# The opening of a hybrid convolution and S5 block: pole constants ahead of x, two modulation slabs summed on GpSimd, two input tiles run channel by channel

## The chip, the cores and the metric

One core of one Trainium2 chip runs the whole kernel. The metric is device time in microseconds (us); lower is better. The median of three runs of the kernel before is 2548.56 us (2545.19 to 2549.18).

## The reference, cut to what matters

```python
c_act = silu(c)
sh1, sc1, g1, sh2, sc2, g2 = split(c_act @ w_ada + b_ada, 6)   # w_ada: 1024 x 6144
h = rmsnorm(x, norm1_g) * (1 + sc1) + sh1                     # x: 2048 x 1024
z = h @ w_in                                                  # to conv, S5 and gate inputs
...
# S5 mixer: constants of each of 32 groups x 64 states
dt = exp(log_dt); mag = exp(dt * a_re)
e_re, e_im = mag * cos(dt * a_im), mag * sin(dt * a_im)
q_re = ((e_re - 1) * a_re + e_im * a_im) / (a_re ** 2 + a_im ** 2)
q_im = (e_im * a_re - (e_re - 1) * a_im) / (a_re ** 2 + a_im ** 2)
bb_re, bb_im = q_re * b_re - q_im * b_im, q_re * b_im + q_im * b_re
x_re, x_im = scan(e_re, e_im, u @ bb)
y_ssm = glu(gelu(x_re @ c_re - x_im @ c_im + d * u))
...
x = x + g1 * (merged @ w_out)                                 # then a SwiGLU FFN and a last rmsnorm
```

Only the part before the first `h @ w_in` (the "opening", the first 60 us or so) is touched. What it must deliver is h for the first 512 tokens, which needs sh1 and sc1 (the first 2048 columns of `c_act @ w_ada`) and the normalized x, and the constants of the S5 mixer.

## The kernel before, in words

The five engines each run a program of their own, in the order in which it is written, and wait for each other on semaphores; nothing is reordered. `Steps` only gives names to semaphore counts. The sequence is worked in four blocks of 512 tokens, and every fp32 product in the projections is made of three fp32r matmuls (`three`): weight and activation are split into a high and a low part. The weights come in chunks of 128 x 1024, through three `raw` buffers; GpSimd splits each into `w_hi` and `w_lo` (a CAST and a subtraction) in one of two slots.

The opening works as follows.

- SP loads eight slabs of `w_ada` of 1 MB each (`SLABS`; slab n holds shift or scale, one half of the 1024 columns, one half of the 1024 rows), then the first three weight chunks, then small things (`load_small`). ACT's queue loads small vectors (`nat_v`), the four tiles of x (`xs`), the S5 poles (`nat_a`), `log_dt`, and B (`nat_b`).
- The modulation is `c_act @ w_ada`, a vector times a matrix. For slabs 1, 3, 5, 6 and 7 PE does it (`modulation_rows`: four fp32 matmuls a slab, into the rows of bank 7). For slabs 0, 2 and 4 DVE sums row by row (`slab_sum`, four instructions a slab, each scaling a 128 x 512 piece by c and adding it to `acc`), and PE adds up the partitions of these sums with two more matmuls (L1800). DVE then copies the rows (`modrow`, L684), PE transposes them (`mt`), and DVE makes `mod` and `scale`.
- ACT takes squares of x (`norm_stats`), the root, and scales x (`nx`).
- DVE makes the arguments of exp, sin and cos for the S5 constants (`jexp`, `jarg`: fifteen short instructions, each waiting for the one ahead of it through `link`), ACT makes exp and sin of them, and DVE works out q in eleven more.
- PE transposes x in eight channel tiles (`h0` to `h7`, four 128 x 128 transposes each); ACT makes `h_hi` and h in the bank (`h_tile`, two instructions a tile), and DVE makes `h_lo` (`h_split`). Then PE starts the first input tile `us0`, all eight channel tiles of it, then `us1`, `us2`, `us3` and the others.
- After the last `h_split` DVE turns B into the scaled B (seven instructions, L727 to L734) and builds `wm` (24 instructions, L739 to L741), which PE needs only after `ug0`, the sixth tile.
- When a tile `us` is done, ACT copies it (`ssm_input`), stores it, and issues eight DMAs for its turned form (`ssm_turn`), in the order us0, us1, turn 0, us2, turn 1, us3, turns 2 and 3, and only then the sigmoid of `ug0` and the copies of the transposed `wm` (`state_matrix`).

## Time and profile before

| | us |
|---|---|
| median of three runs | 2548.56 |
| the profiled execution, its own time | 2551.3 |
| its span | 2549.5 |
| PE busy | 2492.0 (98% of the span) |
| POOL (GpSimd) busy | 1733.5 (68%) |
| DVE busy | 1641.1 (64%) |
| ACT busy | 863.8 (34%) |

The granted TensorE clock has a mean of 0.993 of full speed over the span. PE is busy nearly all the time after the opening, so the table says that the end is set by when PE can start and by what it then has to do. The opening is short and has little PE work that counts: there, which engine waits for which has to be read instruction by instruction. A row of the timeline gives start and duration, engine, line, operation, tiles (out<-in), and in brackets how long the engine sat idle before it and what ended that. `PEld` is the weight load that goes with a matmul. An fp32 matmul shows as two records.

### The profile page before, as it was taken

The page shows a single profiled execution, that of the slowest core. Times are in us where ns is not written, and L with a number is a line of the kernel's source. Part 1 is how long each engine was busy: PE and PEld are TensorE (multiplying, and loading weights), DVE is VectorE, ACT ScalarE, POOL GpSimd, SP SyncE. Part 2 cuts the span into 40 slices and gives each one's busy share as a digit, 9 for nine tenths or more (in the row PEclk, how much of TensorE's full clock was granted, in tenths as well). Part 3 has the DMA queues.
Part 4 walks back from the last instruction along what each step waited for, and adds up shares of the span by engine and source line. Part 5 has one row for each costly group of instructions (what it writes and reads, how often), then busy time and mean ns, then how long its engine had stood idle before and what let it go on. Part 6 is the DMA issues. An engine that isn't in the chain of part 4 may idle for free. (4 is left out here: it accounts for less than half of the span.)

```text
span 2549.5 us, 31364 instructions
## 1 busy us (share of the span) xinstructions
PE 2492.0 (98%) x11419; PEld 2050.3 (80%) x11419; DVE 1641.1 (64%) x2045; ACT 863.8 (34%) x1367; POOL 1733.5 (68%) x1188
## 2 busy tenths in 40 slices
PE   7999999999999999999999999999999999999998
PEld 3888788888888888887788888878888888887886
DVE  5889739945596648947733334385655336889597
ACT  4322411143012421145333345442323334445444
POOL 2776777677866777676887767787787764445444
PEclk9999999999999999999999999999999999999999
DMA  8676347553656347562332232324565337476433
GB/s 279 203 192 215 108 157 223 156 169 107 221 167 190 124 160 220 136 226 83 124 93 81 79 110 93 108 80 152 174 196 184 111 98 251 129 234 205 156 99 116
DMA packets 426161, 395.66 MB, mean 155 GB/s; under 512 B 92232, under 2 KB 330520, under 8 KB 424472
## 3 DMA queue, kind: packets, MB, share of 16 engines
q1 hardware_dynamic: 324112, 317.83, 40.1%
q10 hardware_dynamic: 101896, 75.82, 9.6%
q8 instruction: 92, 1.51, 0.2%
q14 instruction: 61, 0.50, 0.1%
HBM read 317.88 MB, written 67.24 MB: 151 GB/s over the span
## 5 line engine op out<-in xcount | busy, mean ns | idle before, releaser
L2181 POOL TENSOR_TENSOR w_lo<-raw,w_hi 128x1024 fp32r<-128x1024 f32 x192 | 479.4, 2497 | 15.4
L2179 POOL CAST w_hi<-raw 128x1024 fp32r<-128x1024 f32 x192 | 211.8, 1103 | 369.9 <-PE bank L1865 278.4
L1863 PE MATMUL bank<-h_hi,w_hi 128*128 128x512 f32 x896 | 352.2, 393 | 0.9 <-ACT wm L1296 0.9
L1865 PE MATMUL bank<-h_hi,w_lo 128*128 128x512 f32 x896 | 349.8, 390 | 0.0
L1864 PE MATMUL bank<-h_lo,w_hi 128*128 128x512 f32 x896 | 349.5, 390 | 0.0
L829 DVE SCALAR_TENSOR_TENSOR bank<-uc,cwt,bank 128x512 f32<-128x512 f32 x464 | 323.2, 751 | 6.2
L2204 POOL TENSOR_TENSOR fw_lo<-fsum,fw_hi 128x512 fp32r<-128x512 f32 x176 | 235.8, 1343 | 74.1 <-ACT fw_hi L1573 74.0
L1863 PE MATMUL bank<-xc_hi_T,fw_hi 128*128 128x512 f32 x704 | 275.5, 391 | 4.9 <-DVE tr L1024 3.0
L2231 POOL TENSOR_TENSOR ow_lo<-raw,ow_hi 128x512 fp32r<-128x512 f32 x116 | 165.3, 1427 | 162.7 <-ACT ow_hi L1614 162.6
L1865 PE MATMUL bank<-xc_hi_T,fw_lo 128*128 128x512 f32 x704 | 274.2, 389 | 0.0
L1864 PE MATMUL bank<-xc_lo_T,fw_hi 128*128 128x512 f32 x704 | 274.0, 389 | 0.0
L2110 PE MATMUL bank<-ow_hi,hid_hi 128*128 128x512 f32 x616 | 241.3, 392 | 6.2 <-POOL ow_lo L2231 6.2
L2111 PE MATMUL bank<-ow_hi,hid_lo 128*128 128x512 f32 x616 | 241.0, 391 | 0.0
L2112 PE MATMUL bank<-ow_lo,hid_hi 128*128 128x512 f32 x616 | 240.8, 391 | 0.0
L1863 PE MATMUL bank<-xc_hi_B,fw_hi 128*128 128x512 f32 x528 | 207.2, 392 | 5.1 <-DVE xc_lo_B L813 2.4
L2204 POOL TENSOR_TENSOR fw_lo<-raw,fw_hi 128x512 fp32r<-128x512 f32 x110 | 157.9, 1436 | 77.7 <-ACT fw_hi L1573 77.4
L1864 PE MATMUL bank<-xc_lo_B,fw_hi 128*128 128x512 f32 x528 | 206.0, 390 | 0.0
L1865 PE MATMUL bank<-xc_hi_B,fw_lo 128*128 128x512 f32 x528 | 206.0, 390 | 0.0
L1863 PEld LDWEIGHTS bank<-h_hi,w_hi 128*128 128x128 f32 x896 | 169.0, 189 | 36.0 <-issue 1.7
L1865 PEld LDWEIGHTS bank<-h_hi,w_lo 128*128 128x128 f32 x896 | 168.7, 188 | 35.9
L1864 PEld LDWEIGHTS bank<-h_lo,w_hi 128*128 128x128 f32 x896 | 169.0, 189 | 34.5
L1573 ACT ACTIVATE fw_hi<-fsum 128x512 fp32r<-128x512 f32 x176 | 110.8, 629 | 224.1 <-PE bank L1865 114.5
(333 smaller groups left out, 5220.4 us busy)
## 6 DMA issues: line engine op xcount, KB each, us to landing
raw<-in_w_in SPq DMA_DIRECT2D x112, 512.0 KB, 3.9
raw<-in_w_ffn_in SPq DMA_DIRECT2D x66, 512.0 KB, 5.8
hid_scratch<-tr SPq DMA_DIRECT2D x88, 256.0 KB, 3.2
raw<-tsum_scratch SPq DMA_DIRECT2D x66, 256.0 KB, 3.2
g2b<-in_w_ada SPq DMA_DIRECT2D x64, 256.0 KB, 3.7
ssm_m<-vk_scratch SPq DMA_DIRECT2D x32, 512.0 KB, 5.1
raw<-in_ssm_glu SPq DMA_DIRECT2D x32, 512.0 KB, 3.6
raw<-in_w_out SPq DMA_DIRECT2D x32, 512.0 KB, 3.6
```

Source lines behind the costliest of these rows:

```text
L829: ins = v.scalar_tensor_tensor(out=dst, in0=src, scalar=w, in1=conv_bank(m)[:], op0=ALU.mult, op1=ALU.add)
L1573: s.activation(fw_hi[i][:], src, ACT.Copy).then_inc(whi_done, 1)
L1863: t.matmul(dst, wh, xh, start=first, stop=False)
L1864: t.matmul(dst, wh, xl, start=False, stop=False)
L1865: return t.matmul(dst, wl, xh, start=False, stop=last)
L2110: t.matmul(dst, hid_hi[h][:, cols], ow_hi[w][:], start=(k == 0), stop=False)
L2111: t.matmul(dst, hid_lo[h][:, cols], ow_hi[w][:], start=False, stop=False)
L2112: ins = t.matmul(dst, hid_hi[h][:, cols], ow_lo[w][:], start=False, stop=(k == KH2 - 1))
L2179: g.tensor_copy(hi[:], src[:]).then_inc(hi_done, 1)
L2181: g.tensor_tensor(lo[:], src[:], hi[:].bitcast(F32), ALU.subtract).then_inc(split_done, 1)
L2204: g.tensor_tensor(fw_lo[i][:], part[WEIGHTS[i]], fw_hi[i][:].bitcast(F32), ALU.subtract)\
L2231: g.tensor_tensor(ow_lo[n % OW][:], fraw[n % 4][:, 0:HALF], ow_hi[n % OW][:].bitcast(F32), ALU.subtract)\
```

## The change

Six things are done together.

1. On ACT's queue x is loaded last: poles, `log_dt` and B come first.
2. On SP's queue slabs 6 and 7 are moved behind the first two weight chunks.
3. [...] DVE sums slabs 4 and 6. PE multiplies slabs 1, 3, 5 and 7 only, and slab 7 last, behind the two sum rows.
4. DVE works out the S5 constants before anything of the modulation, then slab 4, the mean for the norm, the first two instructions of B, the root, slab 6, and the rest of B; then `modrow`, `mod` and `scale`. ACT makes exp and sin ahead of the squares of x. PE transposes poles and B early.
5. `us0` and `us1` run together, channel tile by channel tile: for each k PE waits for `h_lo` of k, transposes tile k + 2 (the transposed tiles now use two banks), and does the six matmuls of k. The `h_split` instructions stand between those for `wm`.
6. The third weight chunk is split into a third slot, since the first two are now in use until both tiles end.

The diff, cut to its core:

```diff
+        w_hi += early(ync_at, mc_at, ("w_hi_third", [P, CH], F32R))
+        w_lo += early(ync_at + 4096, mc_at, ("w_lo_third", [P, CH], F32R))
+        slot_of = lambda b, w: SPL if (b, w) == (0, 2) else w % SPL
...
-        pe_pro = ["v1", "ada1", "v0", "ada3", "ada5", "ada6", "ada7", "sums", "mt"] + h_steps[0:4] + ["bx"] + h_steps[4:] + ["v2"]
+        pe_pro = ["v1", "v0", "ada1", "bx", "ada3", "ada5", "sums", "ada7"] + h_steps[0:2] + ["mt"] + h_steps[2:] + ["v2"]
...
-        act_pro = ["cs", "dt"] + norm_act + [f"nx{i}" for i in R(TT)] + ["ej", "m8", "sj", "cj"] + h_act
+        act_pro = ["cs", "dt", "ej", "m8", "sj", "cj"] + norm_act + [f"nx{i}" for i in R(TT)] + h_act
...
-            slab_sum(0)
-            slab_sum(2)
-            norm_mean("pro")
-            slab_sum(4)
-            norm_root("pro")
...
+            slab_sum(4)
+            norm_mean("pro")
...
             dve.wait_ge(*tensor.after("pro", "bx"))
             link(v.tensor_tensor(b1[:], first, by_h(qr), ALU.mult))
             link(v.tensor_tensor(ptmp[:], first, by_h(qi), ALU.mult))
+            norm_root("pro")
+            slab_sum(6)
...
                 link(v.tensor_tensor(wm[:, :, s, :], first, by_h(jer[:, j, :]), ALU.mult))
+                if 1 <= s <= 4:
+                    h_split("pro", 2 * s - 2)
                 link(v.tensor_tensor(part, second, by_h(jei[:, j, :]), ALU.mult))
+                if 1 <= s <= 4:
+                    h_split("pro", 2 * s - 1)
...
             modulation_rows(1)
+            parameter_rows()
             modulation_rows(3)
+            modulation_rows(5)
+            pe.wait_ge(slab_pool, 2 * KD - 1)
+            t.matmul(bank[7][0:4, :], one_row[:, 3:7], acc[:, 0:HALF], start=False, stop=False)
+            pe.wait_ge(pro_v, mark["slab6"])
+            t.matmul(bank[7][0:4, :], one_row[:, 2:6], acc[:, HALF:], start=False, stop=False)\
+                .then_inc(*tensor.step("pro", "sums"))
+            modulation_rows(7)
...
+                    for k in R(KD):
+                        pe.wait_ge(*vec.after("pro", f"hl{k}"))
+                        if k + 2 < KD:
+                            transposes("pro", k + 2)
...
+                        for m in R2:
...
+                            ins = three(bank[plan[b, f"us{m}"]][:], hi[:, k, :], lo[:, k, :], h_hi[:, k, :], h_lo[:, k, :],
+                                        k == 0, k == KD - 1)
...
+            def slab_sum(*slabs):
+
+                sums, made = acc[:, 0:HALF], 0
+                for n in slabs:
+                    pool.wait_ge(ada_in[n], 16)
+                    for j in R(KD // 2):
+                        k = SLABS[n][2] * KD // 2 + j
+                        row = ada[n][:, j, :]
+                        g.tensor_tensor(sums if k == 0 else row, row, cact[:, k:k + 1].broadcast_to([P, HALF]), ALU.mult)\
+                            .then_inc(slab_pool, 1)
+                        made += 1
+                        if k:
+                            pool.wait_ge(slab_pool, made)
+                            g.tensor_tensor(sums, sums, row, ALU.add).then_inc(slab_pool, 1)
+                            made += 1
...
+            slab_sum(0, 2)
...
+            for n in R(6):
+                load_slab(n)
...
                     load(b, n, key)
+                    if b == 0 and n == 1:
+                        load_slab(6)
+                        load_slab(7)
```

How this moves the instructions is seen best in three places. The first is PE from its first transpose to its first weight matmul; `ada` is a slab, `xs` is x, `acc` holds the summed slabs. Before:

```order
L1777 MATMUL bank<-ident,nat_v 128x84
L1788 MATMUL bank<-ada_225,zc 4x512 x4
L1777 MATMUL bank<-ident,nat_a 128x64
L1788 MATMUL bank<-ada_227,zc 4x512 x4
L1788 MATMUL bank<-ada_229,zc 4x512 x4
L1788 MATMUL bank<-ada_230,zc 4x512 x4
L1788 MATMUL bank<-ada_231,zc 4x512 x4
L1800 MATMUL bank<-acc,one_row 4x512 x2
L1805 MATMUL bank<-ident,modrow 128x4 x4
L1818 MATMUL bank<-ident,xs 128x128 x16
```

With the change:

```order
L1779 MATMUL bank<-ident,nat_a 128x64
L1792 MATMUL bank<-ada_227,zc 4x512 x4
L1801 MATMUL bank<-ident,nat_b_205 128x32 x16
L1801 MATMUL bank<-ident,nat_b_206 128x32 x16
L1792 MATMUL bank<-ada_229,zc 4x512 x4
L1792 MATMUL bank<-ada_231,zc 4x512 x4
L1810 MATMUL bank<-acc,one_row 4x512
L1812 MATMUL bank<-acc,one_row 4x512
L1792 MATMUL bank<-ada_233,zc 4x512 x4
L1825 MATMUL bank<-ident,xs 128x128 x8
L1833 MATMUL bank<-ident,modrow 128x4 x4
```

One slab of four matmuls is gone, the last slab stands behind both sum rows, and B's transposes fill a place further up.

The second is DVE between the S5 constants and `modrow`, with the change (`sv` holds the constants, 128 x 32 each; before, `modrow` stood right behind the `jarg` instructions and the slabs ahead of them):

```order
L614 SCALAR_TENSOR_TENSOR jarg<-jarg 128x288
...
L703 TENSOR_TENSOR sv<-sv 128x32
L669 TENSOR_SCALAR acc<-ada_230,vt 128x512
L671 SCALAR_TENSOR_TENSOR acc<-ada_230,vt,acc 128x512 x3
L627 TENSOR_SCALAR ss<-ss 128x4
L716 TENSOR_TENSOR b_216<-bank,sv 128x512
L717 TENSOR_TENSOR ptmp<-bank,sv 128x512
L632 RECIPROCAL rs<-sd 128x4
L671 SCALAR_TENSOR_TENSOR acc<-ada_232,vt,acc 128x512 x4
```

Fifteen instructions stand between the first row and the second, and everything that PE's sum row and ACT's norm wait for now stands behind all of them.

The third is GpSimd behind its constants, with the change (before, the first of these rows was the CAST of chunk 0):

```order
L2182 TENSOR_TENSOR acc<-ada_226,vt 128x512
L2182 TENSOR_TENSOR ada_226<-ada_226,vt 128x512
L2187 TENSOR_TENSOR acc<-acc,ada_226 128x512
...
L2187 TENSOR_TENSOR acc<-acc,ada_228 128x512
L2219 CAST w_hi_52<-raw_49 128x1024
L2221 TENSOR_TENSOR w_lo_54<-raw_49,w_hi_52 128x1024
L2219 CAST w_hi_53<-raw_50 128x1024
L2221 TENSOR_TENSOR w_lo_55<-raw_50,w_hi_53 128x1024
L2219 CAST w_hi_third<-raw_51 128x1024
L2221 TENSOR_TENSOR w_lo_third<-raw_51,w_hi_third 128x1024
```

Fifteen instructions now come ahead of the first split, and three splits follow one another where two did.

## Rows read from the trace of the kernel before

**Rows 1.** Timeline of PE in the opening: start us, us, operation [idle before].
```profile
22.51 16.63 PE L1788 MATMUL bank<-ada,zc 128*4 128x512 f32 x32 [4.69 <-DMA ada<-in_w_ada]
38.97 1.88 PE L1800 MATMUL bank<-acc,one_row 128*4 128x512 f32 x4
...
42.03 1.96 PE L1818 MATMUL bank<-ident,xs 128*128 128x128 f32 x16
```

**Rows 2.** Windows: stretch, length, busy of PE, PEld, DVE, ACT, POOL, PEclk, DMA share, GB/s.
```profile
22.50:28.50 6.00, 5.99 (x8) 0.86 (x8) 2.66 (x5) 3.75 (x6) 0.00 (x0) 0.54 1.04 377
28.70:40.80 12.10, 12.10 (x29) 2.32 (x28) 4.88 (x18) 8.26 (x10) 5.33 (x4) 1.00 0.93 294
```

**Rows 3.** Timeline of DVE in the opening.
```profile
26.42 2.33 DVE L663 SCALAR_TENSOR_TENSOR acc<-ada,vt,acc 128x512 f32<-128x512 f32 x3
...
29.11 0.19 DVE L677 TENSOR_TENSOR sv<-sv 128x32 f32<-128x32 f32 x1
...
33.67 0.46 DVE L606 SCALAR_TENSOR_TENSOR jarg<-jarg 128x288 f32<-128x288 f32 x1
40.96 0.68 DVE L684 COPY modrow<-bank 4x512 f32<-4x512 f32 x1 [6.83 <-PE bank L1800]
...
42.62 0.17 DVE L646 TENSOR_TENSOR scale<-scale,vt 128x8 f32<-128x8 f32 x1
```

**Rows 4.** SP's issue of slab 7, and its time from issue to landing.
```profile
16.73 4.46 SPq L2239 DMA_DIRECT2D ada<-in_w_ada  x1
...
DMA to landing us min/median/max: 17.0/17.0/17.0
```

**Rows 5.** Timelines: POOL's first split; ACT behind silu of c, and its last sine.
```profile
35.30 1.04 POOL L2179 CAST w_hi<-raw 128x1024 fp32r<-128x1024 f32 x1 [32.44 <-DMA raw<-in_w_in]
36.42 2.35 POOL L2181 TENSOR_TENSOR w_lo<-raw,w_hi 128x1024 fp32r<-128x1024 f32 x1
...
11.45 1.28 ACT L1279 ACT_TABLE_LOAD   x1
...
36.80 0.52 ACT L1288 ACTIVATE jer<-jarg,half_pi 128x288 f32<-128x288 f32 x1
```

**Rows 6.** Timelines near 110 us: POOL (three rows), then DVE (one).
```profile
107.84 2.40 POOL L2181 TENSOR_TENSOR w_lo<-raw,w_hi 128x1024 fp32r<-128x1024 f32 x1
110.20 3.12 POOL L2161 TENSOR_TENSOR g2b<-g2b,vt 128x512 f32<-128x512 f32 x1
113.27 3.13 POOL L2179 CAST w_hi<-raw 128x1024 fp32r<-128x1024 f32 x1
...
109.02 6.47 DVE L754 SCALAR_TENSOR_TENSOR sin_t<-ktmp,sin_t 128x2080 f32<-128x2080 f32 x2
```

**Rows 7.** Timelines near 181 us: two DVE instructions of 128 x 32, and POOL.
```profile
181.38 0.21 DVE L894 TENSOR_TENSOR carry<-carry,cos_t 128x32 f32<-128x32 f32 x1
181.62 2.28 DVE L896 TENSOR_TENSOR carry<-carry,ctmp 128x32 f32<-128x32 f32 x1
...
181.47 2.39 POOL L2181 TENSOR_TENSOR w_lo<-raw,w_hi 128x1024 fp32r<-128x1024 f32 x1
```

**Rows 8.** By line, whole span: POOL's multiplication and addition (ns min/median/max, first and last start).
```profile
L2161 POOL TENSOR_TENSOR g2b<-g2b,vt x56: 1032/1042/3122, 84.3 to 1124.4; 128x512 f32<-128x512 f32 x56
...
L2169 POOL TENSOR_TENSOR acc<-acc,g2b x64: 1265/1295/2247, 89.7 to 1158.8; 128x512 f32<-128x512 f32 x64
```

**Rows 9.** Groups of DVE instructions, 54.3 to 77 us: busy us, mean ns, idle before.
```profile
L739 DVE TENSOR_TENSOR wm<-bank,jer 128x512 f32<-128x512 f32 x8 | 5.5, 691 | 0.3
```

**Rows 10.** Timeline of ACT when tiles us1 and us2 end.
```profile
62.40 1.12 ACT L1355 ACTIVATE uz<-bank 128x512 f32<-128x512 f32 x1 [4.31 <-PE bank L1865]
...
63.94 3.85 ACTq L1364 DMA_DIRECT2D u<-us_scratch  x8
67.84 1.12 ACT L1355 ACTIVATE uz<-bank 128x512 f32<-128x512 f32 x1 [4.32 <-PE bank L1865]
```

**Rows 11.** Timeline of PE: the first weight matmul.
```profile
50.58 0.76 PE L1863 MATMUL bank<-h_hi,w_hi 128*128 128x512 f32 x1
```

More of the change, by code:

```diff
@@ L442, in build @@
                     plan[st, n] = z % 4
+                    if st == "pro":
+                        plan[st, n] = z % 2
+                    elif st == 0 and n[:2] == "us":
+                        plan[st, n] = (z + 2) % 4
                     z += 1
@@ L553, in build @@
         ada_in = [sem(f"ada_in{s}") for s in R(ADA)]
+        slab_pool = sem("slab_pool")
         pro_v = sem("prologue_vector")
@@ L682, in _ @@
             angles(jarg[:, 0, :, :], jarg[:, 1, :, :], jtmp[:], th, T + 1, "jargs")
-            dve.wait_ge(*tensor.after("pro", "sums"))
-            link(v.tensor_copy(modrow[:], bank[7][0:4, :]), "modrow")
-            dve.wait_ge(*tensor.after("pro", "mt"))
-            rows = lambda a: a.rearrange("p (r j) -> p r j", j=4)
-            link(v.tensor_tensor(rows(mod[:, 0:2 * KD]), bank[7][:, 0:16].rearrange("p (j r) -> p r j", j=4),
-                                 rows(bmod[:, 0:2 * KD]), ALU.add))
-            scale_of(0)
-            flat2 = lambda a: a[:].rearrange("p a b -> p (a b)")
+            link(v.tensor_tensor(t0, ar, ar, ALU.mult))
+            link(v.tensor_tensor(t1, ai, ai, ALU.mult))
+            link(v.tensor_tensor(den, t0, t1, ALU.add))
+            link(v.reciprocal(den, den))
             dve.wait_ge(*scal.after("pro", "cj"))
@@ L735, in _ @@
                                         op0=ALU.mult, op1=ALU.subtract))
+            dve.wait_ge(*tensor.after("pro", "ada7"))
+            link(v.tensor_copy(modrow[:], bank[7][0:4, :]), "modrow")
+            dve.wait_ge(*tensor.after("pro", "mt"))
+            rows = lambda a: a.rearrange("p (r j) -> p r j", j=4)
+            link(v.tensor_tensor(rows(mod[:, 0:2 * KD]), bank[7][:, 0:16].rearrange("p (j r) -> p r j", j=4),
+                                 rows(bmod[:, 0:2 * KD]), ALU.add))
+            scale_of(0)
             for s in R(T):
@@ L1279, in _ @@
             s.activation(sv[:, 2, :], sv[:, 2, :], ACT.Exp).then_inc(*scal.step("pro", "dt"))
-            norm_stats("pro", 64)
-            act.wait_ge(*vec.after("pro", "nr"))
-            for i in R(TT):
-                s.activation(xs[:, i, :], xs[:, i, :], ACT.Copy, scale=rs[:, i:i + 1]).then_inc(*scal.step("pro", f"nx{i}"))
             act.wait_ge(pro_v, mark["jargs"])
@@ L1288, in _ @@
             s.activation(jer[:], jarg[:, 1, :, :], ACT.Sin, bias=half_pi[:, 0:1]).then_inc(*scal.step("pro", "cj"))
+            norm_stats("pro", 64)
+            act.wait_ge(*vec.after("pro", "nr"))
+            for i in R(TT):
+                s.activation(xs[:, i, :], xs[:, i, :], ACT.Copy, scale=rs[:, i:i + 1]).then_inc(*scal.step("pro", f"nx{i}"))
             act.wait_ge(pro_v, mark["scale0"])
@@ L1788, in modulation_rows, with parameter_rows @@
                     ins = t.matmul(bank[7][0:4, :], zc[:, k, 3 - r:7 - r], ada[n % ADA][:, j, :],
[L1789 removed]
+                                   start=(n == 1 and j == 0), stop=(n == 7 and j == KD // 2 - 1))
                 ins.then_inc(*tensor.step("pro", f"ada{n}"))
+            def parameter_rows():
+                pe.wait_ge(bx_in, 64)
+                for n in R(2):
+                    turned = bank[4 + n][:].rearrange("p (g h) -> p g h", h=HG)
+                    for h in R(HG):
+                        ins = t.transpose(turned[:, :, h], nat_b[n][:, :, :, h].rearrange("g a p -> g (a p)"),
+                                          ident[0:G, 0:G])
+                ins.then_inc(*tensor.step("pro", "bx"))
             modulation_rows(1)
[L1793 to L1794 removed]
+            parameter_rows()
             modulation_rows(3)
[L1796 to L1806 removed]
+            modulation_rows(5)
[5 more added lines that the diff above has]
+            modulation_rows(7)
             def wait_bank(stage, name):
@@ L1820, in transposes @@
                 ins.then_inc(*tensor.step(stage, f"h{k}"))
-            for k in R(4):
+            for k in R(2):
                 transposes("pro", k)
-            pe.wait_ge(bx_in, 64)
-            for n in R(2):
-                turned = bank[4 + n][:].rearrange("p (g h) -> p g h", h=HG)
-                for h in R(HG):
-                    ins = t.transpose(turned[:, :, h], nat_b[n][:, :, :, h].rearrange("g a p -> g (a p)"),
-                                      ident[0:G, 0:G])
-            ins.then_inc(*tensor.step("pro", "bx"))
-            for k in R(4, KD):
-                transposes("pro", k)
-            pe.wait_ge(taps_in, 16 * KC)
-            pe.wait_ge(pro_v, mark["scale0"])
-            turn_rows_in(2, nat_w, bank[7])
+            pe.wait_ge(pro_v, mark["modrow"])
+            for j in R(4):
+                ins = t.transpose(bank[7][:, 4 * j:4 * j + 4], modrow[:, j * P:(j + 1) * P], ident[0:4, 0:4])
+            ins.then_inc(*tensor.step("pro", "mt"))
             def state_matrix():
@@ L1881, in layer @@
                     for k in R(kt):
-                        if b == 0 and name == "us0":
-                            pe.wait_ge(*vec.after("pro", f"hl{k}"))
                         ins = three(bank[plan[b, name]][:], hi[:, k, first_col:first_col + P],
@@ L2236, in _, with load_slab @@
         def _(sp):
-            for n, (kind, half, rows) in enumerate(SLABS):
+            def load_slab(n):
+                kind, half, rows = SLABS[n]
                 col = kind * D + half * HALF
```

55 lines of the change are left out of this document (24 added, 31 removed).

## The prediction

> **What bounds the kernel now.** The page says that PE is busy 98% of the span, so the end comes when PE has done its list, and the opening counts by how late PE's weight matmuls begin. I read PE's timeline in the opening first. From the landing of slab 3 at 22.51 us it multiplies slabs and then the two sum rows, until 40.85 [rows 1]. The windows say at which clock: 0.54 of full speed, nearly the lower level of 1.2 GHz, from 22.5 to 28.5 us, behind 4.69 us without work, and the full 2.4 GHz from 28.7 on [rows 2]. Seven whole records in 6.0 us make 0.86 us each at half clock (the eighth is cut by the window's edge), and 28 in 12.1 make 0.43 at full clock. So PE is the bound from 28.7 to 40.85. Then comes DVE's timeline: `modrow` at 40.96, `scale` done at 42.79 [rows 3]. It had idled 6.83 us before `modrow`, and this is the time that the change wants to fill. The first weight matmul starts at 50.58 [rows 11], and ACT takes `us1` at 62.40, when PE is done with it [rows 10]. From there on each step waits for one that began in the opening, so I count the whole shift of that moment as a shift of the end, and look at ACT's list of DMAs for what is added behind it.
>
> The last view is the one that decides: what DVE and POOL (GpSimd) do to each other, where both read SBUF. Before, POOL stands idle until 35.30 [rows 5], so DVE's short instructions in the opening meet nobody. With the change POOL works from 11.5 us on.
>
> **What the two engines do to each other.** Near 110 us, a w_lo ends at 110.24, DVE's two instructions of 128 x 2080 start at 109.02 and take 6.47, and POOL's multiplication takes 3.12 and its CAST 3.13 [rows 6], where 1.04 is the median of the one [rows 8] and the duration of the other alone [rows 5]. That is a strict taking of turns: DVE waits until 110.24, works 2.2, POOL works 1.04, DVE works 2.2, POOL works again. It holds for the shortest ones as well: of two subtractions and products of 128 x 32, one takes 0.21, and the next, which starts 0.15 after a w_lo of 2.39 us has started, takes 2.28 and ends as that one ends [rows 7]. Instructions with an operand in PSUM do not wait: the eight products for wm take 691 ns in the mean with two splits beside them [rows 9].
>
> The Trainium skill, "SBUF — State Buffer", section "SBUF: two separate sides", calls this an exclusive lock on a pair of ports, held for a whole instruction by whichever of the two starts first, and the trace agrees in what it excludes. The page does not say whose turn is next when both wait. Its rule alone would allow that DVE always goes first, which makes the first term below 0, or that POOL runs its whole list first, which gives the same 34 us as turns do. The rows show turns.
>
> **The parts of the change.**
>
> *The S5 arguments (part 4).* Alone, the fifteen instructions take 29.11 to 34.13, 5.0 us [rows 3]. They can start when silu (11.43), a table load of 1.28 [rows 5] and the exp of `log_dt` of 0.23 are over: 13.0 us, against 29.1 before. But POOL starts its list at 11.5: 8 x 1.04 + 7 x 1.27 = 17.2 us [rows 8], of which 1.5 are over at 13.0. One for one, DVE ends at 13.0 + 5.0 + 15.7 = 33.7, and with its last turn about 34. So nothing is won: 34.13 before.
>
> *The rest of the constants.* ACT needs 2.8 us for exp and sine (before, the last ended at 37.32, 3.2 behind the arguments [rows 3, 5]), so about 36.9. DVE's four and eleven short instructions would take 4 us alone. Beside them POOL now does three splits one behind the other, 3 x (1.04 + 2.35) = 10.2 us [rows 5], from 33 to 44.5 with DVE's turns in it. About six of DVE's instructions go in there, and nine more at 0.22 follow: 46.6. Before, these were spread between the `h_split`s and held up nothing. Now slab 4, the mean, the root and slab 6 stand behind them.
>
> *Slab 4, mean, two of B, root, slab 6.* One of 0.5 and three of 0.78 [rows 3], 2.8: 49.4. The mean 0.2, two PSUM instructions 1.45 [rows 9], the root 0.2: 51.3. ACT scales x beside the next step, so PE won't wait for that. Slab 6, 4 x 0.78: 54.4. DMA is not late: slab 7 lands at 16.7 + 17.0 = 33.7 now [rows 4], and two chunks ahead add about 3 us.
>
> *PE (parts 1 to 3).* It does 18 fp32 matmuls and not 22, which is worth 3.4 us only where it is the bound. Now slab 6's row and slab 7 stand behind slab 6's sum: ten records. PE has then been idle for some 20 us but for one row, and 4.69 us of idleness were enough for half clock [rows 1, 2]. Bounds: 10 x 0.43 = 4.3 and 10 x 0.86 = 8.6. As before, I take about seven slow and three fast, 7.3: with latencies, `modrow` at 62.0 and not 40.96. That is **+21.0** (between +18.0 and +22.3).
>
> *The two tiles together (part 5).* Before, 21.4 us from `modrow` to the end of `us1`. Now: `scale` 1.8 behind `modrow`; then four instructions for wm and the first `h_split`, 3.6; then seven more `h_split`s and ten for wm at 0.72, 12.3; then PE's last six matmuls, 1.4, and latency: 19.3, or -2.1. PE has 14 us of work in that time, and idles 3 us or more ahead of it, so part of it runs at half clock: up to 2 us of this gain goes. I take **-1.2** (from -2.1 to 0). With the parts of B moved ahead, wm ends later on DVE's list than before in us, but relative to PE's need early: no cost. The cover is the four tiles until PE transposes it.
>
> *ACT behind the tiles.* `us0` and `us1` now end together. Copy and store take 1.54, twice, and turn 0 takes 3.85: 6.9, while `us2` ends 5.44 behind `us1` [rows 10]. ACT is from there on without a pause until it copies wm's transposes, which PE waits for. So **+1.2** (0 to +1.4).
>
> *At nothing:* the third slot (the split is ready by 45, needed past 65), the moved small loads, x last (I expect it in by about 25 us, and ACT comes to it at 37).
>
> Sum: 21.0 - 1.2 + 1.2 = +21.0 on the profiled execution's 2551.3, which gives 2572.3. It is 2.7 above the median of 2548.56, so for the median I say 2569.5.
>
> **The rivals.** The resolution of such a measurement is about 0.2%, 5.1 us.
>
> *Rival 1, DVE goes first: no change that can be told.* If the short instructions slip in between POOL's, which has a wait ahead of each addition, the arguments are ready at 18 us, slab 4 is summed by 28.9, and slab 6, landed at 34.2, by 37.3. Ten records at full clock put `modrow` at 42.0, +1.0; seven slow ones +4.0, as PE idles from 32 to 37. With the two other terms: +1 to +4, a median of 2549.6 to 2552.6. For it: the gaps are there. Against it: rows 6 and 7, where DVE's next instruction came 0.03 us behind its last and still lost the turn. Between it and my forecast lies all where DVE wins some of the turns, up to +14.
>
> *Rival 2, the other side: PE's shorter list decides.* With x behind everything on ACT's queue, the slabs could get the DMA engines earlier. If slab 7 is in by 33 us and slab 6 summed by 34, `modrow` comes up to 3.4 us earlier, and the tiles give 2.1: -5.5, 2543. It needs DVE free of waiting besides, and decides only if slab 7 lands no later than now, with 1 MB of chunks put ahead of it. The GB/s of 377 in the window beside which slabs 3 to 5 land [rows 2] say that there is no room to spare.
>
> *Rival 3, the wait is longer.* Every record at half clock, and all short instructions behind a w_lo each: +25, 2573.6.
>
> **How the numbers follow.** My forecast with its neighbour rival 3 gets 0.83, its own range 2562 to 2575; the part-way cases and rival 1 get 0.12, of which 0.09 end within 0.2%; rival 2 gets 0.05. The range goes from 2551 to 2575, which takes in half of rival 1. Slower by over 0.2% 0.86, within 0.2% 0.09, faster 0.05.
>
> **What would show it.** In the new profile: the 128 x 32 instructions of DVE between 13 and 45 us at 1.2 to 2.5 us each and not 0.19; `jarg` done near 34; slab 6 summed near 54; `modrow` near 62; PE idle between 33 and 54 and at half clock behind it; ACT's first `uz` near 83. Wrong if the short ones show 0.2 beside a busy POOL, or if `modrow` comes before 45.

## The result, and the profile after

The changed kernel takes 2564.72 us in the median of 7 runs (2555.92 to 2571.28), the kernel before 2546.33 (7 runs of the same session, 2543.77 to 2549.18): a ratio of 1.0061, 95% interval [1.0047, 1.0075]. It is slower: by 15.5 us if one goes by the ratio, by 18.4 if by the two medians. The profiled execution of it took 2559.61 us, with a span of 2557.8; that is only 8.3 us above the profiled execution before (2551.3), and the last section says where the other microseconds went.

The timeline of the changed kernel shows how GpSimd (POOL) and DVE took turns from the first argument on, where before the same fifteen instructions had stood alone [rows 3]. The rows are start us, us, operation, and in brackets the idle time before and what ended it.

```profile
13.14 0.52 DVE L680 TENSOR_TENSOR sv<-sv 128x32 f32<-128x32 f32 x1 [0.23 <-ACT sv L1281]
13.70 1.58 POOL L2187 TENSOR_TENSOR acc<-acc,ada 128x512 f32<-128x512 f32 x1
13.70 0.46 DVE L681 TENSOR_TENSOR jexp<-iota_f,sv 128x288 f32<-128x288 f32 x1
14.19 1.14 DVE L683 TENSOR_TENSOR sv<-sv 128x32 f32<-128x32 f32 x1
15.24 1.03 POOL L2182 TENSOR_TENSOR ada<-ada,vt 128x512 f32<-128x512 f32 x1
15.36 0.95 DVE L601 TENSOR_SCALAR sv<-sv 128x32 f32<-128x32 f32 x1
16.35 0.18 DVE L602 TENSOR_SCALAR sv<-sv 128x32 f32<-128x32 f32 x1
16.36 1.30 POOL L2187 TENSOR_TENSOR acc<-acc,ada 128x512 f32<-128x512 f32 x1
16.57 1.14 DVE L603 SCALAR_TENSOR_TENSOR sv<-sv 128x32 f32<-128x32 f32 x1
...
26.52 1.46 DVE L614 SCALAR_TENSOR_TENSOR jarg<-jarg 128x288 f32<-128x288 f32 x1
...
35.07 2.38 POOL L2221 TENSOR_TENSOR w_lo<-raw,w_hi 128x1024 fp32r<-128x1024 f32 x1
35.28 2.21 DVE L697 TENSOR_TENSOR sv<-jei,sv 128x32 f32<-128x32 f32 x1
...
41.63 0.48 DVE L669 TENSOR_SCALAR acc<-ada,vt 128x512 f32<-128x512 f32 x1
...
46.13 3.08 DVE L671 SCALAR_TENSOR_TENSOR acc<-ada,vt,acc 128x512 f32<-128x512 f32 x4
...
49.27 1.87 PE L1812 MATMUL bank<-acc,one_row 128*4 128x512 f32 x2 [16.59 <-DVE acc L671]
...
50.93 4.64 PE L1792 MATMUL bank<-ada,zc 128*4 128x512 f32 x8
...
55.67 0.68 DVE L729 COPY modrow<-bank 4x512 f32<-4x512 f32 x1 [2.68 <-PE bank L1792]
...
61.92 0.45 PE L1825 MATMUL bank<-ident,xs 128*128 128x128 f32 x1 [5.00 <-DVE h_lo L622]
```

A DVE instruction of 128 x 32 starts just behind a POOL instruction and ends just behind its end: 14.19 to 15.33, while POOL's addition ends at 15.28. It then lasts 1 us and not 0.2. One that meets a gap of POOL slips in: at 16.35 the multiplication has ended at 16.27, the addition behind it waits on its semaphore, and DVE needs its 0.18. Of the fifteen, eleven took 0.95 to 1.46, the first took 0.52 and not 0.19, as it met the end of a multiplication, and three slipped in (0.46, 0.18, 0.18). So `jarg` was done at 27.98 (34.13 before). The rest of the constants met the three splits; the slowest took 2.21 to 2.49 us, two of them in place of 0.19, some 2.0 us of waiting behind a w_lo. Slab 4 came at 41.63, slab 6 was summed at 49.21, PE had idled 16.59 us, and `modrow` stands at 55.67, 14.7 us later than before.

The windows of the changed kernel (stretch, length, busy of PE, PEld, DVE, ACT, POOL, granted clock, DMA share, GB/s) show the clock at its lower level of 1.2 GHz behind this idle time, and again behind the 5.00 us before the first `h_lo`.

```profile
48.00:52.00 4.00, 2.73 (x4) 0.48 (x5) 3.83 (x6) 2.51 (x3) 0.00 (x0) 0.50 1.04 303
52.00:56.00 4.00, 4.00 (x12) 0.98 (x11) 1.28 (x3) 0.00 (x0) 0.00 (x0) 0.87 0.50 150
...
60.00:64.00 4.00, 2.08 (x7) 1.91 (x8) 3.86 (x7) 1.78 (x4) 0.00 (x0) 0.50 0.00 0
```

ACT's timeline, against [rows 10]: both tiles arrive at once, at 77.50 (62.40 before), and the second copy and its store stand ahead of turn 0. The sigmoid of `ug0`, which followed in this list at 85.36 before, starts at 101.59: 16.2 us later.

```profile
77.50 1.10 ACT L1357 ACTIVATE uz<-bank 128x512 f32<-128x512 f32 x1 [2.14 <-PE bank L1864]
...
79.02 1.11 ACT L1357 ACTIVATE uz<-bank 128x512 f32<-128x512 f32 x1 [0.42 <-ACT uz L1357]
...
80.64 3.75 ACTq L1366 DMA_DIRECT2D u<-us_scratch  x8
84.43 1.11 ACT L1357 ACTIVATE uz<-bank 128x512 f32<-128x512 f32 x1 [4.31 <-PE bank L1864]
```

Not all of it reaches the wait of PE for the mean of `dt`, which stands in every kernel: it begins at 258.72 before and at 272.19 after, 13.5 us later, and 13.3 us are left at 1698 us. From the sigmoid to this wait the two kernels run the same lists, and DVE's is what PE waits for. PE also waited for `ys_lo`, the output of the S5 part, before; after, no such wait stands there. The third row is from the kernel of the second experiment, which is described below:

```profile
245.97 0.50 PE L1863 MATMUL bank<-ys_hi,w_hi 128*128 128x512 f32 x1 [2.32 <-DVE ys_lo L614]
...
261.14 0.39 PE L1862 MATMUL bank<-ys_hi,w_hi 128*128 128x512 f32 x1
...
263.88 0.80 PE L1864 MATMUL bank<-ys_hi,w_hi 128*128 128x512 f32 x1 [2.32 <-DVE ys_lo L623]
```

It is tempting to say that a late PE finds DVE ready and so wins the wait back. The third row speaks against it: that kernel is 18.1 us late at the sigmoid and has the whole wait of 2.32 us. What differs is the length of DVE's list. The first `ys_lo` instruction starts 155.2 us behind the sigmoid before, and 152.0 us behind it after, because DVE meets POOL's splits at other points of its list; all of this difference arises between 63 and 99 us behind the sigmoid, in DVE's instructions that meet a split. One such place in the timelines of DVE and POOL, first before, then after:

```profile
149.85 2.72 POOL L2181 TENSOR_TENSOR w_lo<-raw,w_hi 128x1024 fp32r<-128x1024 f32 x1
150.24 2.88 DVE L866 TENSOR_TENSOR wst<-wst,cos_t 128x512 f32<-128x512 f32 x1
...
165.36 1.30 POOL L2219 CAST w_hi<-raw 128x1024 fp32r<-128x1024 f32 x1 [7.69 <-PE bank L1864]
165.68 1.52 DVE L869 TENSOR_TENSOR wst<-wst,cos_t 128x512 f32<-128x512 f32 x1
```

Over all twelve profiles this goes in steps and not with the lateness. In five of them (the changed kernel and the third, fifth, sixth and eighth experiment, from 1.6 to 16.2 us late at the sigmoid) the first `ys_lo` instruction starts 152.0 to 152.1 us behind the sigmoid and PE does not wait. In the other seven it starts 155.0 to 157.8 us behind, and PE waits 2.31 us or more. What decides which case a kernel gets was not tested. So in the experiments I read three things beside the median: when the sigmoid of `ug0` starts, which only the opening sets, how far PE is at the wait for `dt`, and the difference of the two, which varies by 4 us between these kernels (170.6 to 174.6 us) though no edit touches the stretch between them. What the last third adds differs too; it is told at the end.

### The profile page after: what moved, and what is told of

Same layout as the page of the kernel before. It is cut to its first block and busy times, and to the rows that moved or that the text cites. A ratio compares the mean times of both kernels' runs of the same rounds, so it can differ in the third digit from the quotient of the medians.

```text
span 2557.8 us, 31364 instructions
## 1 busy us (share of the span) xinstructions
PE 2489.5 (97%) x11411; PEld 2049.1 (80%) x11411; DVE 1669.6 (65%) x2041; ACT 862.7 (34%) x1366; POOL 1747.5 (68%) x1203
```

## The experiments

**e1_pe_sums: PE's sums in place of POOL's.** PE multiplies slabs 0 and 2 too, and POOL is idle until its first split. All else is as in the changed kernel.

```diff
+            modulation_rows(0)
+            modulation_rows(2)
             modulation_rows(3)
             modulation_rows(5)
-            pe.wait_ge(slab_pool, 2 * KD - 1)
-            t.matmul(bank[7][0:4, :], one_row[:, 3:7], acc[:, 0:HALF], start=False, stop=False)
...
-            slab_sum(0, 2)
```

> The changed kernel, but PE multiplies slabs 0 and 2 as well, and GpSimd does nothing before its first weight split. The order on DVE is as in the change. Theory (the two engines exclude each other, and DVE's short instructions wait for a GpSimd instruction each): DVE's fifteen argument instructions take 5 us again and are done by 18.5 us and not 28.0; the constants are done by about 25 us and not 41.6; slab 4 is summed at 28.5 (it lands at 25.5), slab 6 lands near 34 and is summed by 38 to 40 because its four instructions now meet the weight splits; modrow near 44 to 46 and not 55.7; time 5 to 8 us above the kernel before, 9 to 12 below the changed one. Rival (the order does it: the constants stand ahead of slab 4 whatever GpSimd does): the arguments are still done near 28, modrow stays above 53 and the time within 3 us of the changed kernel's. Second rival (PE's additional eight records cost): slab 6 early, but modrow late behind PE.

Measured: 2550.22 us (10 runs) beside 2545.8 of the kernel before (13 runs), 1.0024 [1.0011, 1.0036]. The timeline of its DVE:

```profile
13.14 0.19 DVE L680 TENSOR_TENSOR sv<-sv 128x32 f32<-128x32 f32 x1 [1.11 <-ACT sv L1281]
...
17.70 0.46 DVE L614 SCALAR_TENSOR_TENSOR jarg<-jarg 128x288 f32<-128x288 f32 x1
...
33.48 5.90 DVE L671 SCALAR_TENSOR_TENSOR acc<-ada,vt,acc 128x512 f32<-128x512 f32 x4 [3.39 <-DMA ada<-in_w_ada]
...
44.00 0.68 DVE L729 COPY modrow<-bank 4x512 f32<-4x512 f32 x1 [0.84 <-PE bank L1792]
```

The arguments are done at 18.16, `modrow` is 11.7 us earlier than in the changed kernel, and the expected steps came as expected. But slab 6, four instructions that take 3.08 alone, takes 5.90: it comes behind the weight chunks and meets their splits. So `modrow` is still 3.0 us later than before. The sigmoid is 5.0 us late (90.32) and the wait for `dt` 6.2, behind a wait for `ys_lo` of 6.85 us.

**e2_pool_for_nobody: POOL works for nobody.** As the last, but POOL runs its fifteen instructions all the same; its products go to a place that nothing reads, and so do its sums.

```diff
-                        row = ada[n][:, j, :]
+                        src, row = ada[n][:, j, :], dead[:]
...
-                        g.tensor_tensor(sums if k == 0 else row, row, cact[:, k:k + 1].broadcast_to([P, HALF]), ALU.mult)\
+                        g.tensor_tensor(sums if k == 0 else row, src, cact[:, k:k + 1].broadcast_to([P, HALF]), ALU.mult)\
```

> As e1, but GpSimd still runs its eight multiplications and seven additions, reading slabs 0 and 2 and writing to a dead buffer; no engine waits for a result of them (PE makes the row itself; DVE waits for their end only where they are long over). Theory: it is the working of GpSimd and not its results that costs, so DVE's arguments are done near 28 to 30 us again, the constants near 42, modrow within 2 us of the changed kernel's 55.7, and the time 14 to 19 us above the kernel before. Rival (lateness of the GpSimd sums, or the order on PE): as e1, about 5 to 8 above before.

Measured: 2560.02 us (4 runs), 1.0059 [1.0044, 1.0074]. Here nobody needs POOL's results, PE has its full list, and yet the short instructions take a microsecond each:

```profile
14.21 1.13 DVE L684 TENSOR_TENSOR sv<-sv 128x32 f32<-128x32 f32 x1
...
46.56 3.08 DVE L672 SCALAR_TENSOR_TENSOR acc<-ada,vt,acc 128x512 f32<-128x512 f32 x4
...
57.15 0.68 DVE L730 COPY modrow<-bank 4x512 f32<-4x512 f32 x1 [3.73 <-PE bank L1794]
```

So it is POOL's being at work, and not a late result of it, that costs 13.2 us at `modrow`, 13.1 at the sigmoid, 11.7 at the wait for `dt` and 9.8 in the median, all against the first experiment.

**e3_slabs_first: slabs 6 and 7 first.** The changed kernel with part 2 undone.

```diff
-            for n in R(6):
+            for n in R(8):
                 load_slab(n)
...
-                    if b == 0 and n == 1:
-                        load_slab(6)
-                        load_slab(7)
```

> The changed kernel with slabs 6 and 7 loaded ahead of the weight chunks again; all else as in the change. Theory: the splits can't start before chunk 0 lands near 34.5 to 35 and not 30, so GpSimd stands idle from 30.3 to 35 and some eight of DVE's short constants pass unhindered: constants done by 35 to 37 and not 41.6, slab 4 by 38 to 41 (its instructions now meet splits), slab 6 by 44 to 47 and not 49.2; modrow 2 to 5 us earlier than 55.7, the time 2 to 6 us below the changed kernel's. Rival (the place of the slabs on the queue is only a matter of DMA landing): slab 7 is 2.6 us earlier but nobody waits for it, so no change beyond 1 us.

Measured: 2558.02 us (4 runs), 1.0048 [1.0033, 1.0063]; `modrow` at 55.34, only 0.3 earlier than in the changed kernel. The constants were done at 34.66, 7 us earlier, since they met no split. But then the splits met slab 4 (timeline of DVE and POOL):

```profile
34.67 1.04 POOL L2219 CAST w_hi<-raw 128x1024 fp32r<-128x1024 f32 x1 [4.74 <-DMA raw<-in_w_in]
34.70 1.29 DVE L669 TENSOR_SCALAR acc<-ada,vt 128x512 f32<-128x512 f32 x1
...
35.79 2.40 POOL L2221 TENSOR_TENSOR w_lo<-raw,w_hi 128x1024 fp32r<-128x1024 f32 x1
36.02 6.90 DVE L671 SCALAR_TENSOR_TENSOR acc<-ada,vt,acc 128x512 f32<-128x512 f32 x3
```

Slab 4 was summed at 42.92, against 38 to 41 expected, and slab 6 at 49.16, against 44 to 47: the expectation had the splits meet slab 4, but at too low a price, and left out that they reach slab 6 too (3.87 us and not 3.08). The sigmoid and the wait for `dt` are where the changed kernel has them (101.56 and 272.15). What DVE and POOL both had to do here stood in one row, whichever came first.

**e4_pe_kept_busy: PE kept busy.** The changed kernel, with 70 matmuls of 128 x 128 that nobody reads ahead of the wait for slab 6, and 22 behind the transposes of `modrow`.

```diff
+            for _ in R(70):
+                t.matmul(bank[3][:, 0:P], ident[:], mean_w[:], start=True, stop=True)
             pe.wait_ge(pro_v, mark["slab6"])
```

> The changed kernel with idle PE filled: 70 matmuls of 128 x 128 into an unused bank behind the first sum row, and 22 more behind the transposes of modrow. Theory (part of the loss is half clock behind PE's idle time): the granted clock is 1.00 from 36 us on, slab 6's row and slab 7 take 4.5 us and not 6.3, modrow near 54, and the two tiles end about 2 us earlier relative to it: time 3 to 5 us below the changed kernel's. If the dummies overrun (they take 15 us at full clock and there are 16.6 to fill) it gains less. Rival (the clock costs nothing since DVE sets the pace): no change.

Measured: 2562.3 us (4 runs), 1.0064 [1.0048, 1.0081]. PE's timeline:

```profile
49.45 1.02 PE L1814 MATMUL bank<-acc,one_row 128*4 128x512 f32 x2 [0.74 <-DVE acc L671]
...
50.30 3.60 PE L1792 MATMUL bank<-ada,zc 128*4 128x512 f32 x8
```

Ten records take 4.4 us and not 6.3, `modrow` comes at 54.01, and both tiles end at 73.64, 3.9 us earlier. So the idle time's price in clock is 3.9 us there, and the sigmoid is 4.7 us earlier (96.88). At the wait for `dt` only 1.9 us are left (270.25), since DVE's list has its longer form again, with a wait for `ys_lo` of 2.31 us. The median cannot be told from the changed kernel's 2564.72, which was measured in another session.

**e5_tiles_alone: part 5 by itself.** The kernel before with part 5 only, and part 6, which it needs: `first_inputs`, two banks for transposes, the third slot.

```diff
-                    ssm_input(*R(KS))
+                    first_inputs()
+                    ssm_input(2, 3)
```

> The kernel before with part 5 alone (us0 and us1 channel by channel, two banks for the transposed tiles, third slot for the third chunk); everything ahead of modrow is as before, and the h_splits stay between the short instructions of the constants. Measured so far: in the kernel with PE's sums the end of us1 stood at modrow + 21.4 us, as before, but ACT's sigmoid of ug0 came 2.0 us later against it. Theory (the two tiles together gain on PE what ACT loses behind them): modrow at 41.0, us1 done at about 61 (before 62.4), the sigmoid within 0.8 us of before's 85.4, median within 1.5 us of the kernel before. Rival (part 5 is what costs the rest): ACT's queue behind the two tiles moves everything behind it by 2 us or more, the sigmoid at 87.4 or later and the median 2 us or more above before. Second rival (it is worth its own -1.2 and more, and only the late modrow hid it): the sigmoid at 84 or earlier, median 1.5 us or more below.

Measured: 2545.63 us (12 runs) beside 2547.70 (35 runs), 0.9996 [0.9982, 1.001]: no change that can be told. ACT's timeline:

```profile
62.93 1.10 ACT L1362 ACTIVATE uz<-bank 128x512 f32<-128x512 f32 x1 [2.16 <-PE bank L1867]
```

`modrow` is at 41.06 as before, the tiles end 0.5 us later than `us1` did, not 1.4 earlier, and the sigmoid is 1.6 us late: between the theory and the rival. PE's clock was 0.64 and 0.51 of full speed from 44 to 52 us (1.00 and 0.57 before). PE all the same reaches the wait for `dt` 1.2 us early, since DVE's list has its shorter form, without a wait for `ys_lo`; that is no gain of part 5 that these runs show.

**e6_slab6_on_dve: slab 6 on DVE.** The kernel before, with slab 6 summed by DVE behind its arguments, where it had idled.

```diff
             angles(jarg[:, 0, :, :], jarg[:, 1, :, :], jtmp[:], th, T + 1, "jargs")
-            dve.wait_ge(*tensor.after("pro", "sums"))
+            slab_sum(6)
+            dve.wait_ge(*tensor.after("pro", "ada7"))
```

> The kernel before, but slab 6 is summed by DVE behind its S5 arguments (in the 6.83 us in which it idled ahead of modrow) and no longer multiplied by PE; both sum rows stand ahead of slab 7. GpSimd is idle until 35 us, as before. Theory (PE's list from 28.7 us on is what sets modrow, and DVE is free there): eight records of 0.43 us less on PE, modrow 2.5 to 3.4 us earlier (37.6 to 38.5), the sigmoid as much earlier, and as DVE, whose list sets PE's wait near 245 us, moves with it, a median 2.5 to 3.5 us below before, 2542.3 to 2543.3. Rival (the slabs' landing sets it): slab 7 lands at 33.7 and slab 6 not much before, DVE ends slab 6 at 37.3 and slab 7's four matmuls come behind, some at half clock: modrow at 40 to 42, no gain.

Measured: 2556.04 us (12 runs), 1.0033 [1.002, 1.0047]. Both the theory and its rival missed; `modrow` came at 47.40. The timeline of DVE, POOL and PE:

```profile
34.50 5.73 DVE L663 SCALAR_TENSOR_TENSOR acc<-ada,vt,acc 128x512 f32<-128x512 f32 x4
...
35.66 1.27 POOL L2180 CAST w_hi<-raw 128x1024 fp32r<-128x1024 f32 x1 [32.81 <-DMA raw<-in_w_in]
...
37.02 2.66 POOL L2182 TENSOR_TENSOR w_lo<-raw,w_hi 128x1024 fp32r<-128x1024 f32 x1
...
40.28 1.87 PE L1801 MATMUL bank<-acc,one_row 128*4 128x512 f32 x2 [6.61 <-DVE acc L663]
...
41.94 5.35 PE L1789 MATMUL bank<-ada,zc 128*4 128x512 f32 x8
```

Only the first of the four instructions is over before the split starts; then they take turns, PE idles 6.61 us, and its ten records then take 7.0 us, against 4.4 with PE kept busy. The free time of DVE in the kernel before was only in part free: from 35.30 on POOL was at work in it.

**e7_pe_sums_slabs_first: PE's sums, and slabs first.** The first experiment with part 2 undone as well (the diffs are those two).

> As e1_pe_sums (GpSimd sums nothing, PE multiplies slabs 0 and 2), and in addition slabs 6 and 7 are loaded ahead of the first weight chunks again. Theory (in e1_pe_sums slab 6 on DVE met the three splits, at 0.75 to 2.7 us an instruction, because it came after the chunks; slabs first, it meets none): slab 6 summed by 34 us and not 39.4, slab 7 done near 37.5, modrow at 38 (e1_pe_sums 44.0, before 41.0), the sigmoid 5 to 6 us earlier than in e1_pe_sums, median 4 to 6 us below it, about 2545. Rival (as where slabs first won 0.3 us with GpSimd's sums in place): the splits move earlier too and meet slab 4 or 6 all the same, modrow at 42 or later.

Measured: 2547.56 us (12 runs), 1.0007 [0.999, 1.0023]. Slab 6 is summed from 30.93 to 34.04 and meets nobody; `modrow` is at 39.09, 1.9 us earlier than before, but the tiles end at 62.93: PE idles 6.41 us for the first `h_lo`, behind two `scale` instructions of 0.82 and 0.94 us that meet a split and four for `wm`, and its matmuls then run at half clock. PE's list of 24 matmuls for slabs is now the bound: slab 7 had landed at 33.44. The sigmoid is 3.4 us ahead of e1_pe_sums, where 5 to 6 had been expected; at the wait for `dt` this kernel is 4.8 us ahead of it, and 1.4 us behind the kernel before.

**e8_h_first: the h_splits ahead of wm.** The last, with this:

```diff
+            for k in R(KD):
+                h_split("pro", k)
             for s in R(T):
...
-                if 1 <= s <= 4:
-                    h_split("pro", 2 * s - 2)
```

> As e7_pe_sums_slabs_first, and DVE's eight h_splits stand ahead of the instructions for wm and not between them. Theory (PE's channel-by-channel tiles wait for the h_split of each channel, which stands behind one or two wm instructions of 0.7 us, the first behind four): us1 ends at modrow + 17 us and not + 21.4, ACT's sigmoid comes 3 to 4.5 us earlier than in e7_pe_sums_slabs_first, wm ends as late as there and PE, which needs it only behind ug0, does not wait for it; median 3 to 4 us below e7_pe_sums_slabs_first, some 4 us below the kernel before. Rival (ACT's two instructions a channel set the pace, not DVE's): us1 ends at modrow + 20 or more, a gain below 1.5 us.

Measured: 2546.78 us (12 runs), 0.9996 [0.9983, 1.0008]. `modrow` at 41.59: PE's clock had fallen to 0.66 from 20 to 24 us, which it had not in the same list of the last kernel. The tiles end 21.6 us behind `modrow`; in the last kernel that was 23.8. The gain is 2.3 us and not 4.4, and PE still idles 5.08 us and starts at half clock. The end of the tiles at `modrow` + 20 or more was the sign of the rival, which laid it to ACT's two instructions a channel; the next experiment fills the idle time. With `modrow` 2.5 us later, the sigmoid comes at 87.16, 0.3 us later than in the last kernel and not 3 to 4.5 earlier.

**e9_slab0_filled: slab 0 on DVE, PE kept busy.** The last, with slab 0 summed by DVE while ACT makes exp and sine, and 20 matmuls for nobody between the transposes of `modrow` and the first `h_lo`.

```diff
+            slab_sum(0)
             dve.wait_ge(*scal.after("pro", "cj"))
...
-            modulation_rows(0)
...
             ins.then_inc(*tensor.step("pro", "mt"))
+            for _ in R(20):
+                t.matmul(bank[3][:, 0:P], ident[:], mean_w[:], start=True, stop=True)
```

> As e8_h_first, with two edits: DVE sums slab 0 in the 2.8 us in which it waits for ACT's exp and sine (18.1 to 20.9), so that PE multiplies five slabs and not six, and PE runs 20 matmuls of 128 x 128 that nobody reads between the transposes of modrow and the first h_split, so that it does not idle there (5.08 us, clock at its lower level for the first matmuls behind). Theory: PE's list of slabs was the bound of modrow in e7_pe_sums_slabs_first (39.1, with slab 7 landed at 33.4), so modrow comes at 37 to 38; the first channels of us0 and us1 run at 0.23 us a matmul and not 0.43, so both tiles end at modrow + 19.5 and not + 21.6: 57.5 (before 62.4); ACT's sigmoid 3 us earlier than before's 85.4 (1.2 of it lost behind the tiles), DVE's first uc 2.5 to 3 us earlier than before's 134.25; median 2 to 4 us below the kernel before. Rival (the slabs set it, or the clock falls all the same): modrow at 39 or later or tiles at modrow + 21 or more, median within 1.5 us.

Measured: 2542.28 us (12 runs) beside 2547.20 (23 runs), **0.9978 [0.9963, 0.9992]**. It beats both kernels. Its windows:

```profile
24.00:28.00 4.00, 4.00 (x6) 0.60 (x5) 3.50 (x9) 3.91 (x7) 0.00 (x0) 0.53 1.05 409
...
48.00:52.00 4.00, 4.00 (x24) 3.33 (x23) 1.42 (x3) 3.12 (x5) 0.00 (x0) 1.00 1.03 324
```

The first half of the expectation missed: `modrow` at 40.47, not 37 to 38, with the clock at 0.61 and 0.53 of full speed from 20 to 28 us. The second held: with the full 2.4 GHz behind it, the tiles end at 59.57, `modrow` + 19.1, and the sigmoid starts at 82.57, 2.8 us earlier than before. So it was the clock, and not ACT, that had held the tiles at `modrow` + 21.6: 2.5 us of it. PE is 4.2 us early at the wait for `dt`.

**e10_tiles_apart: the tiles apart.** The last, with part 5 undone and four transposes ahead of `modrow`'s.

```diff
-                    first_inputs()
-                    ssm_input(2, 3)
+                    ssm_input(*R(KS))
```

> As e9_slab0_filled, but part 5 is undone: us0 first and us1 behind it, four transposed banks, two slots for the weight chunks; the transposes of channels 0 to 3 stand ahead of modrow's, and the h_splits stay ahead of wm. Theory (tile by tile costs PE little and gives ACT its time: us0 done 5.4 us ahead of us1, so that ACT has copied it and issued its turn before us1 is done): modrow at 37 to 38, first weight matmul near 46, us1 done at 57, the sigmoid 5 us earlier than before's 85.4 and uc 5 us earlier than before's 134.25, median 3.5 to 5.5 us below the kernel before and 1 to 2 us below e9. Rival (the two tiles together are worth more than ACT loses): us1 done 1.5 us later than in e9 or more, median above e9's.

Measured: 2550.87 us (12 runs), 1.0007 [0.9991, 1.0022]. `modrow` is at 39.60 and the sigmoid 2.4 us early, not 5: `us0` cannot start before all eight transposed tiles are made, and these wait for ACT's two instructions of a tile, 1.33 us together. Its first weight matmul is at 50.05, and `us1` ends at 61.22, 1.65 us later than in the last kernel. So the rival's sign came: with PE at full clock, channel by channel brings the end of the tiles 1.65 us forward, of which ACT leaves 0.4 at the sigmoid (82.57 against 82.98). PE is 1.5 us early at `dt`, against 4.2; 2.3 us of this difference arise behind the sigmoid. The median's distance of 8.6 us from the last kernel cannot be laid to the edit alone: of the two profiles' distance of 9.0 us, 6.2 arise behind 1685 us.

## Why the prediction was right, and where it was off

It said slower, 2569.5 us, for the reason that decided: that DVE and POOL exclude each other. The second experiment shows this reason alone at work. The median was 4.8 us below the forecast, but the profiled execution, for which the sum was made, was 12.7 us below it (2559.61 against 2572.3). This is how its steps stand.

- *The arguments, 34.* They were done at 28.0. The step that failed is "One for one, DVE ends at 13.0 + 5.0 + 15.7": it made DVE wait for the whole of POOL's list, and added DVE's own time on top. Neither came. At 27.98 the last two of POOL's fifteen instructions were not yet done, 2.3 us by their durations alone. And a turn of both engines took hardly longer than POOL's part of it: from 21.34 to 27.61 five turns took 1.25 us each, where POOL's two kinds of instruction take 1.04 and 1.27. My estimate from these durations is that, of the 14.8 us from 13.14 to 27.98, POOL's work fills 13.3, so that only 1.5 of DVE's 5.0 show. The gaps of rival 1 exist, but only three of the fifteen instructions went into one.
- *The rest of the constants, 46.6.* 41.6. The 6 us of the step above, and one of them lost again: ACT's exp and sine were ready at 30.75, so that the constants met all three splits from the first w_lo on (2.49, 2.21 and 2.22 us in one instruction beside each w_lo).
- *Slab 4 to slab 6, 7.8.* 7.6: from 41.63 to 49.21.
- *Ten records on PE, 7.3.* 6.3. With the clock at its upper level they take 4.4 in the kept-busy experiment, so at 0.43 us more for a slow one some four or five of them were slow, not seven.
- *`modrow`, +21.0.* +14.7, below the lower bound of +18.0. Of the 6.3 us between, 5.0 stand at the end of the constants (the first step, less what was lost again), 0.2 in the slabs and 1.0 in PE's records.
- *The two tiles, -1.2.* +0.4: 21.8 us from `modrow` to the end of both, against 21.4. The step took at most 2 us for the clock; with the clock kept up these tiles end 19.6 us behind `modrow`, close to the 19.3 that the prediction had worked out ahead of this discount.
- *ACT behind them, +1.2.* +1.1 (16.2 at the sigmoid, 15.1 at the tiles' end).
- *"I count the whole shift of that moment as a shift of the end."* It did not hold. Of 16.2 us at the sigmoid, 13.5 are left at the wait for `dt`, because DVE's list between the two, whose end PE waits for, was 2.7 us shorter in this execution: it met POOL's splits at other points. The kernel of the second experiment, without this luck, was 18.1 us late at the sigmoid and 17.9 at the wait for `dt`.

The sum by the measured steps is 14.7 + 0.4 + 1.1 = 16.2, of which 13.5 are left at the wait for `dt` and 13.3 at 1698 us. In the two profiled executions only 8.3 are left at the end, since the one before happens to have a PE wait of 4.42 us in its last third that the other has not. The medians say 15.5 by the ratio and 18.4 by their difference. So the reason and the sign were right, but that +21.0 came this near to the medians is partly luck: the opening was too dear in it by 4.8 us at the sigmoid (+21.0 against +16.2), and how far the medians lie from the 13.3 us at 1698 us is decided in the last third, of which it says nothing.

In one reading the prediction took too little: beside the eight products for wm with an operand in PSUM stood four splits, not two (57.06 to 76.90 us), and they still took 691 ns in the mean.

Rival 2, that PE's shorter list decides, was out of reach in the changed kernel. Its condition was never met: the earliest `modrow`, 39.09, is that of the seventh experiment, whose list of slabs on PE is longer than before (24 matmuls and 20), and with the 20 of the ninth it came at 40.47, behind a slower clock.

Of the change's six parts, these are the prices found. POOL's sums (part 3) cost 11.7 us at `modrow` in the first experiment. Slabs behind the chunks (part 2) cost 4.9 more once these are gone (44.00 against 39.09). Part 5 alone is worth nothing that can be told with the h_splits where they were, and 1.65 us at the end of the tiles with PE kept busy, 0.4 of it at the sigmoid. With parts 1 and 4, poles and B ahead of x and the constants first, slab 6 is done ahead of the splits in the seventh experiment; with the arguments behind slabs 0, 2 and 4, in the sixth, it is not. That these two parts help by themselves was not tried.

## What to carry to other kernels

Before you give work to an idle GpSimd, list what VectorE does at that time out of SBUF: each of its instructions, however small, may have to wait for a whole one of GpSimd's. Here a chain of fifteen short ones met eleven waits of nearly a microsecond and took 14.8 us and not 5.0. An idle stretch of VectorE was worth something here only where GpSimd was idle too. And an idle TensorE paid twice, once for the wait and once for the clock behind it: matmuls that nobody reads, in a wait that cannot be removed, brought the two tiles forward by 3.9 us in the changed kernel, though only 1.9 of it reached the wait for `dt` and nothing that can be told the median. With GpSimd's sums gone as well, they were part of the one kernel that beat the one before. Last, a shift of the opening is not the shift of the end: later lists can come out shorter or longer by some microseconds, and two single profiles do not show which part of their distance is the change.

## What the runs showed of the hardware that I had not expected

**Who gets the turn is not fixed.** In the last third of the kernel before, POOL waits for its turn through nine of DVE's instructions (timeline of POOL, DVE and PE):

```profile
2352.87 6.48 POOL L2231 TENSOR_TENSOR ow_lo<-raw,ow_hi 128x512 fp32r<-128x512 f32 x1 [4.14 <-ACT ow_hi L1614]
...
2353.34 0.68 DVE L1137 TENSOR_TENSOR quarter_c<-quarter_a,quarter_c 128x512 f32<-128x512 f32 x1
...
2359.40 0.79 PE L2110 MATMUL bank<-ow_hi,hid_hi 128*128 128x512 f32 x1 [4.42 <-POOL ow_lo L2231]
```

In the kernel of the ninth experiment the same place goes turn by turn:

```profile
2352.79 1.69 POOL L2270 TENSOR_TENSOR ow_lo<-raw,ow_hi 128x512 fp32r<-128x512 f32 x1 [4.15 <-ACT ow_hi L1615]
...
2353.25 1.78 DVE L1139 TENSOR_TENSOR quarter_c<-quarter_a,quarter_c 128x512 f32<-128x512 f32 x1
2354.95 1.79 DVE L1050 TENSOR_TENSOR hid_lo<-quarter_c,hid_hi 128x512 fp32r<-128x512 f32 x1
```

POOL's instruction takes 6.48 us in the one and 1.69 in the other. PE's wait of 4.4 us stands in the profiles of three kernels (the one before, the sixth and the tenth experiment), whose way from about 1685 us to PE's last wait takes 842.2, 845.8 and 846.4 us; in the nine others, without it, the same way takes 834.8 to 840.2. None of these kernels touches this stretch. I take it that most of the spread of a kernel's own runs (2541.51 to 2555.03 for the kernel before in one session) comes from such turns, here and in DVE's list ahead of `ys_lo`; that was not tested. The prediction's rule of strict turns is the usual case in these traces and not a law. The Trainium skill, "SBUF — State Buffer", section "SBUF: two separate sides", says what excludes what, and these runs agree with it: in the first experiment four sums with both operands in SBUF took 5.90 us beside splits and not 3.08, and a product with an operand in PSUM, beside the w_lo at 38.91, took 0.70. Whose turn comes next no run here settles.

**The clock falls in one kernel and not in the other.** PE has nearly the same list from 12 to 28 us in the six kernels with PE's sums, and the profile shows it busy throughout from 20 to 28. The granted clock there was 1.00 in two of them (e7 and e10) and between 0.50 and 0.92 in the other four. All that I see ahead of it is that PE came to B's transposes at 17.15 and 17.32 us in the two, and between 17.68 and 18.86 in the four; the eight records of slab 1 before them took 5.21 and 5.54 us in the two and 5.92 to 6.56 in the four. It costs up to 2.5 us of `modrow` (39.09 against 41.59); what decides it stays open.
